# A decoder layer in one program block: w_o tile by tile, with the router's steps between the halves

## The reference, cut to what matters

```
z  = rmsnorm(h) @ w_in                   # u 512 | v 512 | q 512 | k 128 | v_b 128
ya = gelu(u) * (tril(W_s[g]) @ layernorm(gelu(v)) + b_s[g])     # chunks of 128 positions
yb = sliding-window attention(q, k, v_b) # window 128, 8 query heads, 2 key heads, sinks, ALiBi
h  = h + [rmsnorm(ya) | rmsnorm(yb)] @ w_o
hn = rmsnorm(h)
logits = hn @ w_router + b_router        # 32 experts; the 4 largest; softmax over these
h  = h + sum over the 4 chosen experts of gate * (clamped_swiglu(hn @ w_gu[e] + b_gu[e]) @ w_dn[e] + b_dn[e])
h  = h + sigmoid(rmsnorm(h) @ w_ple_gate) * (p @ w_ple_proj)
y  = rmsnorm(h)
```

## Time and profile before

| | us |
|---|---|
| median of three runs (1558.61 to 1562.68) | 1561.44 |
| the profiled execution | 1555.33 |
| its span, first to last instruction | 1553.7 |
| TensorE busy | 1463.9 (94%) |
| VectorE busy | 1228.6 (79%) |
| ScalarE busy | 1040.6 (67%) |
| GpSimd busy | 183.2 (12%) |
| chain that ended last: TensorE's share | 76% |

### The profile page before, as it was taken

The page is one execution under the profiler, slowest core; times in us unless marked ns, Lnnn a source line. Parts: engine busy times, 40 slices in busy tenths (PEclk is TensorE's granted clock), DMA queues, the critical chain, the costliest instruction groups (busy, mean ns, idle before and its releaser), DMA issues.

```text
span 1553.7 us, 21012 instructions
## 1 busy us (share of the span) xinstructions
PE 1463.9 (94%) x6907; PEld 1212.4 (78%) x6907; DVE 1228.6 (79%) x1024; ACT 1040.6 (67%) x980; POOL 183.2 (12%) x237
## 2 busy tenths in 40 slices
PE   5999599289999999999999999999999999999898
PEld 5887487168888888888888888888888888888676
DVE  4144734759888889999888888999988888898775
ACT  4365522257777777777777777777777777777645
POOL 6000000511011111110111101111011111010000
PEclk9999799589999999999999999999999999999999
DMA  9012055369999999999999999999999999998631
GB/s 320 23 63 82 1 217 195 96 254 387 374 376 376 366 370 378 362 375 368 374 370 375 373 365 371 369 373 373 369 370 380 369 370 381 360 386 287 228 125 42
DMA packets 109065, 465.90 MB, mean 300 GB/s; under 512 B 19058, under 2 KB 24698, under 8 KB 76266
## 3 DMA queue, kind: packets, MB, share of 16 engines
q1 hardware_dynamic: 93978, 445.24, 75.6%
q0 software_dynamic: 14432, 18.94, 3.5%
q10 hardware_dynamic: 624, 1.31, 0.3%
HBM read 457.50 MB, written 24.96 MB: 311 GB/s over the span
## 4 chain that ended last, share of the span: by engine, by line
PE 76%; DVE 2%; ACT 1%; DMA 1%; issue 0%; DVEq 0%; POOL 0%; SPq 0%; ACTq 0%; POOLq 0%
PE bank L2081 30%; PE bank L2084 15%; PE bank L2102 15%; PE bank L2107 7%; PE bank L78 4%; PE bank L2073 2%; PE bank L2052 2%; PE bank L2063 2%; DMA w_slot<-in_w_dn 1%; DVE wg_lo L2008 0%; DVE h_in L1968 0%; PE bank L2165 0%; ACT wg_hi L1825 0%; DMA xg<-hn_rows,idx_in 0%; ACT pair_hi L1680 0%
## 5 line engine op out<-in xcount | busy, mean ns | idle before, releaser
L1862 DVE TENSOR_TENSOR pair_lo<-w_slot,pair_hi 128x2048 fp32r<-128x2048 f32 x384 | 870.5, 2288 | 114.5 <-ACT pair_hi L1680 114.5
L1680 ACT ACTIVATE pair_hi<-w_slot 128x2048 fp32r<-128x2048 f32 x384 | 737.0, 1921 | 262.6 <-PE bank L2084 175.2
L2081 PE MATMUL bank<-pair_hi,xg_hi 128*128 128x512 f32 x1024 | 274.6, 390 | 0.8 <-issue 0.8
L2084 PE MATMUL bank<-pair_lo,xg_hi 128*128 128x512 f32 x1024 | 273.9, 389 | 0.0
L2081 PE MATMUL bank<-pair_hi,xg_lo 128*128 128x512 f32 x1024 | 273.9, 389 | 0.0
L2081 PEld LDWEIGHTS bank<-pair_hi,xg_hi 128*128 128x128 f32 x1024 | 192.7, 188 | 41.7 <-issue 1.5
L2081 PEld LDWEIGHTS bank<-pair_hi,xg_lo 128*128 128x128 f32 x1024 | 192.5, 188 | 40.1
L2084 PEld LDWEIGHTS bank<-pair_lo,xg_hi 128*128 128x128 f32 x1024 | 192.2, 188 | 39.9
L2102 PE MATMUL bank<-pair_hi,aT_hi 128*128 128x512 f32 x496 | 135.7, 395 | 0.0
L2107 PE MATMUL bank<-pair_lo,aT_hi 128*128 128x512 f32 x496 | 133.0, 390 | 0.0
L2102 PE MATMUL bank<-pair_hi,aT_lo 128*128 128x512 f32 x496 | 132.9, 390 | 0.0
(11 more groups left out here) (301 smaller groups left out, 1426.5 us busy)
## 6 DMA issues: line engine op xcount, KB each, us to landing
w_slot<-in_w_gu SPq DMA_DIRECT2D x256, 1024.0 KB, 7.0
w_slot<-in_w_dn SPq DMA_DIRECT2D x128, 1024.0 KB, 7.1
raw<-in_w_in SPq DMA_DIRECT2D x3, 2048.0 KB, 22.6
y_in<-expert_rows SPq DMA_DIRECT2D x3, 2048.0 KB, 10.2
raw<-in_w_o SPq DMA_DIRECT2D x2, 2048.0 KB, 9.3
raw<-in_w_ple_gate SPq DMA_DIRECT2D x2, 2048.0 KB, 11.0
uq<-in_x_prompt SPq DMA_DIRECT2D x4, 512.0 KB, 8.3
h_rows<-uq SPq DMA_DIRECT2D x4, 512.0 KB
```

What stands on the lines that cost most here:

```text
L1680: nc.scalar.activation(pair_hi[pair(b, k)][:], w_slot[k + down][:], ACT.Copy).then_inc(hi_ready, 1)
L1862: mine(nc.vector.tensor_tensor(pair_lo[pair(b, k)][:], w_slot[k + down][:], pair_hi[pair(b, k)][:].bitcast(F32), ALU.subtract), lo_ready)
L2081: nc.tensor.matmul(bank[:, n, :], x[:, c, :], w_hi[:, n * CB:(n + 1) * CB], start=False, stop=False)
L2084: last = nc.tensor.matmul(bank[:, n, :], xg_hi[:, c, :], w_lo[:, n * CB:(n + 1) * CB], start=False, stop=c == KC - 1)
```

## The change

The three blocks become one: there is no point between attention and expert loop at which all engines meet. All names of the later blocks are defined ahead of it, with new places in memory.

Attention is shifted by one tile: `scores(0)` now stands ahead of the first v product, and each later unit stands one tile earlier against the input products. The norms of v move forward with it (`v_norm(4)` ahead of `scores(6)`, and so on), and the squares of y are taken in part between the units (`y_squares(t, j)`, j the mixer). Gating runs in two calls, three tiles and then one (`gated`).

All four halves of w_o are on chip at once (`MIX_HALF`), so that the product runs tile by tile: `mixed(t, n)` for the four halves n of tile t. The steps of the router stand between the halves: positions two tiles back, turning h one tile back, router product one tile back. The residual x comes in rows (four loads, each tile's own buffer, the sample's into the first one). The loads of expert 0 move: pieces 2 and 3, then 0 and 1 behind the splits of w_o, pieces 4 to 7 after the last h, and the four of w_dn once the gate table is done (`routed`) and POOL's scatters have landed (`scattered`). The router's constants are made and loaded after the last scores. The first fetch no longer waits for the bias load; the bias product takes two rows of ones and bias instead of 128, and the bias rows are not zeroed any more. The gate softmax and the gate table now stand between the first splits of the expert loop. The counts for extra blocks are written to bank 1; the line that reads them is unchanged and reads bank 6.

```diff
-                    nc.tensor.matmul(bank[:, n, :], ones_r[:], bias_sb[:, n * CB:(n + 1) * CB], start=True, stop=False)
+                    nc.tensor.matmul(bank[:, n, :], ones_r[0:2, :], bias_sb[0:2, n * CB:(n + 1) * CB], start=True, stop=False)
-            mine(nc.vector.memset(bias_sb[:].bitcast(F32), 0.0))
```

More of the change, by code:

```diff
@@ new lines, in _ @@
+            pool.wait_ge(xg_clear, 1)
+            for i in range(2):
+                pool.wait_ge(hn_stored[i], 16 * len(range(i, TILES, 2)))
+            fetch(0)
+            bias(0)
+            pool.wait_ge(xg_landed, 16)
+            fetch(1)
+            bias(1)
+            fetch(2)
+            bias(2)
+            fetch(3)
+            store(0)
+            with pool.Fori(2, nb - 1) as b:
+                bias(b + 1)
+                fetch(b + 2)
+                store(b - 1)
+            store(nb - 2)
@@ L486, in _ @@
+            store(nb - 1)
         @block.scalar
@@ L629, in _ @@
             read(3, 1)
[L630 to L633, removed]
             act.wait_ge(s_by_pe, S_SUMMED)
@@ new lines, in turn, with ahead @@
+            def turn(b, down):
+                if down:
+                    a_hi(b - 1)
+                for k in range(PAIRS, 8):
+                    hi(b, k)
+                if down:
+                    for k in range(8, 11):
+                        hi(b, k)
+                gate(b)
+                if down:
+                    hi(b, 11)
+                x_hi(b + 1)
+            def ahead(b):
+                for k in range(PAIRS):
+                    hi(b, k)
+            act.wait_ge(mix_done, 2 * TILES)
@@ new lines, in _ @@
+            last.then_inc(kT_banked, 1)
+            both(1, 1)
+            turn_q(0)
+            both(1, 2)
+            turn_q(1)
+            turn_wsp(0)
+            both(1, 3)
+            turn_q(2)
+            turn_wsp(1)
+            both(1, 4)
+            turn_q(3)
+            scores(0)
+            both(2, 0)
+            turn(0)
+            scores(1)
+            z(2, 1, 0)
+            values(0)
+            z(2, 1, 1)
+            turn(1)
+            scores(2)
+            z(2, 2, 0)
@@ new lines, in route @@
+            def route(t):
+                R = ROWS[t]
+                if t == 0:
+                    pe.wait_ge(router_landed, 48)
+                else:
+                    pe.wait_ge(logit_read, t)
+                pe.wait_ge(hnT_ready, t + 1)
+                for c in range(KC):
+                    last = nc.tensor.matmul(bank[0:R, 6, 0:E], hnT[t % 2][:, c, 0:R], w_r[:, c, :],
+                                            start=c == 0, stop=c == KC - 1)
+                last.then_inc(logit_done, 1)
```

1768 lines of the change are left out of this document (841 added, 927 removed).

## The result

The changed kernel takes 1534.32 us (median of four runs, 1533.91 to 1537.17) against 1560.03 before: ratio 0.9838, 95% interval 0.9823 to 0.9853, so 25.7 us less. The forecast was 1529.1, with 1516 to 1551 around it.

A forecast was written before the change was run, and what follows sets the result against it. TensorE was taken to bound the expert loop, so all gain lies ahead of 318 us: 6.8 + 17.9 - 21.4 + 30.0 - 1 = 32.3 us, giving 1529.1 us against the median of the runs; range 1516 to 1551.

The forecast's parts named there:

- lost in the loop and the end: Expert loop: moved w_dn loads cost 1 us (0 to 11.4), two-row bias products nothing (0.1 us each way).
- Attention, and the way to w_o: Front: input products end 6.8 us earlier (0 to 7); from there to the first w_o product 17.9 won (12 to 20).
- another wait takes the hole over: Attention stage: the low end of the first term, where the earlier end of the input products wins nothing.
- the rival that the attention stage ends no earlier: Attention: the hole only moves, 6.8 us less gain, 1536, inside the range; no chance of its own given.
- The mixing stage: Products with w_o plus TensorE's router work: 77.4 us instead of 56.0, ends 70 and 86.
- the two waits in tile 1: Mixing stage: TensorE waits about 1.1 us for turning y of tile 4 and 1.8 for turning h of tile 0.
- the rival of waits at every tile: Mixing stage: router steps in tiles 1 to 4 find inputs late, about 4 us each; gain 12, 1549; chance 0.11.
- that of the lower clock: Mixing stage: small products and short waits keep TensorE at 1.2 GHz, 46 us more; all of it 1575; chance 0.06.
- The way to the experts: Last mixed product to first expert product: 31.4 us instead of 61.4, 30.0 won (24 to 33).
- the index load would pay for w_dn: First gather: if w_dn loads were issued first, it would pay as the second does (index wait 6.6, not 2.2).
- The step that failed: Expert loop's bias products: two rows instead of 128 take the same time, so nothing; ends 0.1 us each way.
- Late weights: Loop's first blocks: DMA sets them, 11.4 us lost instead of 1, first gather pays 6; gain 16, 1545; chance 0.10.

The follow-up runs named there:

- full_rows: The changed kernel with the bias products over 128 rows again, the other bias rows zeroed by ScalarE before the loop: 1524.05 us, ratio to before 0.9772.
- full_rows_early_zero: As full_rows, but the bias tile lies where the turned y lay and is zeroed behind the last router step without two waits: 1520.06 us, ratio 0.9738.
- before_two_rows: The kernel before with only the bias products cut from 128 rows to 2: 1576.51 us, ratio 1.0110.
- before_shift_own_key_wait: The kernel before with attention one tile earlier and a semaphore of its own for the keys' window: 1556.03 us, ratio 0.9966.

## Why the prediction was right, and where it was not

By its own marks, in us of the profiled executions:

```
                                        before    forecast    measured
end of the input products               178.65       171.8       171.8
from there to the first w_o product       21.9         4.0         3.6
the mixing stage                          56.0        77.4        73.7
from there to the first expert product    61.4        31.4        30.9
first expert product stands at          318.04       284.6       280.0
lost in the loop and the end                 -         1.0        17.5
gain                                         -        32.3        20.5
```

*Attention, and the way to w_o.* The two sums came out (25.1 us together, 24.7 forecast), but they are one step and not two: alone, the shift won 1.1 us, and 5.3 with a semaphore of the keys' own. The prediction asked only whether another wait takes the hole over and named none; the wait for the values' window did, with 1.53 us and no loss of clock in this execution. That the input products still end where they were forecast is luck, for two reasons. The prediction carried the gate products' 4.9 us over from before, where they ran at a granted clock of 0.68 behind the wait of 1.11 us; in the changed kernel they run at 1.00 (3.67 us in their row, 5.22 in the earlier trace rows), and the 1.5 us pay for the new hole. Their stretches, before and after:

```profile
167.80:172.70 4.90, 4.90 (x18) 4.06 (x18) 4.71 (x10) 0.00 (x0) 0.00 (x0) 0.68 0.02 3
160.00:163.30 3.30, 3.30 (x19) 2.91 (x17) 2.40 (x7) 0.72 (x2) 0.00 (x0) 1.00 0.45 160
```

And the end of the input products moves from one execution to the next: turning y starts at 171.82 here, but at 172.5 to 176.2 in the five other profiled kernels with the same front. In full_rows, one of them, the hole of 1.72 us was followed by half clock (0.61 from 94 to 97), and its first w_o product stood at 179.43. The time alone (1534) would fit the rival that the attention stage ends no earlier (1536) better than the forecast; in this execution the marks rule it out.

*The mixing stage* kept its 240 products and took the router steps in, with the two waits in tile 1 that were forecast: 1.72 us for turning y of tile 4 (1.1 forecast) and 0.37 for turning h of tile 0 (1.8), none from tile 2 on, one dip of the clock (0.98 over the stage). The term was 3.7 us too dear. Taken apart from start to start in the timeline, 0.8 of it lies in these waits, 1.85 in turning h and the router products (10.15 for the 12), 0.9 in the position products and 0.4 in turning y; the 240 products with their dip took 58.4 for 58.1. The rival of waits at every tile and that of the lower clock have not come true; for the latter the Trainium skill (Perfetto Trace Analysis, Matmul Optimizations) had spoken, and the 0.98 speaks against it here.

*The way to the experts* was right to half a microsecond: the tokens stood at 275.5, 26.4 us behind the last mixed product (26.9 forecast). By parts, small misses cancel: the last write ends at 15.8 (15.3 forecast), the index load starts 2.5 later (4), it and its wait take 2.9 (2.8) and the gather 5.2 (4.7). That the index load would pay for w_dn was a bound and not needed.

*The step that failed* is the one that said of the bias products: "products over 8 rows and over 128 rows take the same, 0.63 and 0.64 for two, so nothing; ends 0.1 us each way". The durations are the same in the loop too (1.19 and 1.17 for four). What they leave out is the distance to the groups on either side: 0.42 us per block, 13.0 for 31 blocks, and 14.3 in the time of full_rows_early_zero. That the time still comes out near the forecast is luck: the error of 16.5 us in the loop shows as only 5.2 in the time (1529.1 against 1534.3), because two others cover it: the front won 4.7 us more than forecast, and the profiled execution of before was 6.1 us under the median that the gain was taken from, while that of the changed kernel is at its median (1534.55 and 1534.32). With the rows' 14.3 in the sum the forecast would have been 1543, 9 us too slow.

The Trainium skill (TensorEngine Tiling (Array Packing), Tiling Modes, Key Properties) says that changing the tiling mode, a mode having 128, 64 or 32 rows, drains the engine, with no figure. The runs agree as far as they go: 64 rows cost as much as two, and two more changes cost the same again. That products over fewer rows, with no tiling meant, are such a change of mode is my reading; the traces show the cost and no drain. It was the rule that spoke against this change, and the prediction did not weigh it.

*Late weights*: not so. In the changed loop no wait of TensorE for a weight is in the trace (from 280 to 1386 it waits 3.0 us, once, for the low part of block 1's tokens, and 0.5 ahead of the first product), and with 128 rows the period is that of before to 0.01 us, with the moved loads in place.

*What stays open*: 2.6 of the 17.5 us are not the rows' (from the first expert product to the end it is 1235.7 us before, 1253.2 in the changed kernel and 1238.3 in full_rows_early_zero). 2.5 of them lie in block 0 (32.1 us long in both kernels with this front, 29.6 before). There the clock comes up at 283.9 in the changed kernel and at 285.5 with 128 rows, but at 317.8 before, 4.2 us behind the start of the turning instead of 8.4 and 9.5 (granted clock 0.52 from 282 to 284, 0.63 from 284 to 286, and 0.56 from 316 to 318). I had held the two rows to be the cause; full_rows_early_zero contradicts it, before_two_rows speaks for it (block 0 is 31.8 us long there, and the clock comes up at 320.8, 7.5 us behind the start of the turning), and why before came up so early was not found. Nor does a run take the front apart beyond the shift of attention: what the single block, the moved loads and the mixing tile by tile are worth is read from the marks of one pair of executions.

## What to carry to other kernels

A product over fewer rows is not free because its own duration is the same: read the starts of the groups on both sides of it, count the changes of shape per turn of the loop, and multiply. An edit off to the side of a change, made in passing, took back more than a third of what the front had won, and it shows in no view of waits, only in the period of the loop. When work moves earlier, list for each moved step every semaphore that it waits on, and ask whether what it counts will have landed by then.

## What was not expected of the hardware

The change from 128 rows to 64 or 2, and back, costs TensorE some 0.2 us each (periods 35.37, 35.79 and 36.17 for none, two and four changes). The clock of the attention stage also falls without a hole: in before_shift_own_key_wait it is 0.79 from 118 to 126, although TensorE is busy for all 8.00 us there and for all 8.00 ahead of it; in the changed kernel the clock is 1.00 over both stretches, with TensorE as busy (68 instructions in the first, where this run had 67). A hole of 1.53 us at 94 (and one of 1.90 in full_rows_early_zero) was followed by full clock in one execution and one of 1.72 us by half clock in another, so that kernels with the same front have their first w_o product anywhere between 175.4 and 179.8.
